# Cached attention keys: loaded in 128-byte runs and turned in 32x32 blocks on VectorE, in place of full transposes on TensorE

## What is computed

```python
def gather_pages(pool, page_table):      # pool: (n_phys, 128, 8 heads, 64)
    pages = pool[page_table]             # page_table: (8 sequences, 2 pages)
    b, n, p, h, d = pages.shape
    return pages.reshape(b, n * p, h, d)
...
k_all = jnp.concatenate([past_k.astype(dt), k_c], axis=1)     # 256 cached + 4 new positions
...
s = jnp.einsum('bhqd,bhqskd->bhqsk', qi, kg).astype(F32) * scale
p = jax.nn.softmax(s.reshape(B, H, qb, -1), axis=-1).reshape(s.shape)
return jnp.einsum('bhqsk,bhqskd->bhqd', p.astype(vg.dtype), vg)
```

## Time and profile before

| | us |
|---|---|
| three timed runs, median (lowest to highest) | 1137.73 (1137.03 to 1140.92) |
| profiled execution, span from first to last instruction | 1136.4 |
| TensorE busy | 1104.2 (97%) |
| VectorE busy | 696.0 (61%) |
| ScalarE busy | 353.0 (31%) |
| SP: cached keys, 32 DMAs of 256 KB, median to landing | 3.1 |

### The profile page before, as it was taken

How to read it: one execution, slowest core, us unless ns; L and a number is a source line. 1 busy time by engine, 2 the same in 40 slices (tenths; PEclk the granted TensorE clock), 3 DMA queues, 4 the chain that set the end, 5 groups by cost and what they waited for, 6 DMA issues and landing times.

```text
span 1136.4 us, 23106 instructions
## 1 busy us (share of the span) xinstructions
PE 1104.2 (97%) x8920; PEld 891.8 (78%) x8920; DVE 696.0 (61%) x1577; ACT 353.0 (31%) x809; POOL 129.3 (11%) x215
## 2 busy tenths in 40 slices
PE   7999999999999899999999999999999998999998
PEld 6778777768777598899977778777777876888997
DVE  4675546766666445567556673766667646463856
ACT  1242223322334153310323332233223332534013
POOL 0211402020211000000001123111102011000000
PEclk9999999999999999999999999999999998999999
DMA  8733236421513674454356331654134147544431
GB/s 262 222 112 117 58 102 211 100 75 40 137 52 112 179 264 150 139 164 131 110 157 177 112 99 41 189 164 94 39 91 117 58 129 237 187 152 149 149 112 42
DMA packets 162327, 148.57 MB, mean 131 GB/s; under 512 B 41512, under 2 KB 144526, under 8 KB 162028
## 3 DMA queue, kind: packets, MB, share of 16 engines
q1 hardware_dynamic: 156820, 135.99, 40.2%
q0 software_dynamic: 2848, 7.79, 2.0%
q10 hardware_dynamic: 2552, 3.32, 0.9%
HBM read 135.42 MB, written 11.07 MB: 129 GB/s over the span
## 4 chain that ended last, share of the span: by engine, by line
PE 88%; DVE 4%; SPq 2%; DMA 2%; issue 1%; ACT 1%; DVEq 0%; ACTq 0%
PE psum L1305 43%; PE psum L1346 10%; PE psum L1367 7%; PE psum L1233 5%; PE psum L1557 2%; PE psum L1574 2%; PE psum L1421 1%; PE psum L1432 1%; PE psum L1693 1%; SPq L1159 1%; DMA arena<-conv_in 1%; PE psum L1959 1%; PE psum L1908 1%; PE psum L1777 1%; PE psum L1938 1%
## 5 line engine op out<-in xcount | busy, mean ns | idle before, releaser
L1305 PE MATMUL psum<-x_b,ring 128*128 128x288 f32 x928 | 245.3, 414 | 0.0
L1305 PE MATMUL psum<-x_a,ring 128*128 128x288 f32 x928 | 243.8, 412 | 0.0
L1305 PEld LDWEIGHTS psum<-x_b,ring 128*128 128x128 f32 x928 | 171.4, 191 | 49.4 <-issue 6.5
L1305 PEld LDWEIGHTS psum<-x_a,ring 128*128 128x128 f32 x928 | 170.6, 191 | 49.0 <-issue 6.5
L2044 ACT ACTIVATE arena<-psum 128x512 f32<-128x512 f32 (+7 forms) x181 | 78.1, 451 | 172.6 <-PE psum L1233 62.7
L1305 PE MATMUL psum<-z,ring 128*128 128x288 f32 (+1 forms) x384 | 83.5, 368 | 0.0
L1305 PEld LDWEIGHTS psum<-z,ring 128*128 128x128 f32 x384 | 62.3, 190 | 12.8 <-issue 2.3
L2044 ACT ACTIVATE arena<-arena 128x256 f32<-128x256 f32 (+9 forms) x102 | 44.5, 465 | 62.5 <-DVE arena L3308 28.2
L1233 PE MATMUL psum<-consts,arena 128*128 128x128 f32 (+2 forms) x362 | 53.9, 281 | 7.3 <-DMA arena<-in_x_prompt 4.9
L1233 PEld LDWEIGHTS psum<-consts,arena 128*128 128x128 f32 (+2 forms) x362 | 42.9, 145 | 17.6 <-issue 6.3
L2044 ACT ACTIVATE triangles<-psum 128x512 f32<-128x512 f32 (+2 forms) x48 | 24.7, 515 | 77.2 <-PE psum L1557 58.8
(11 more groups left out here) (478 smaller groups left out, 1988.8 us busy)
## 6 DMA issues: line engine op xcount, KB each, us to landing
ring<-in_w_in SPq DMA_DIRECT2D x72, 1024.0 KB, 5.4
ring<-in_w_branch SPq DMA_DIRECT2D x12, 1024.0 KB, 5.7
arena<-in_cache_k SPq DMA_DIRECT2D x32, 256.0 KB, 3.1
arena<-in_cache_v SPq DMA_DIRECT2D x32, 256.0 KB, 3.7
ring<-in_w_out SPq DMA_DIRECT2D x8, 1024.0 KB, 5.1
ring<-in_w_pg SPq DMA_DIRECT2D x8, 1024.0 KB, 5.2
arena<-in_state_dn SPq DMA_DIRECT2D x8, 512.0 KB, 6.8
out_dn_sample<-arena POOLq DMA_DIRECT2D x8, 512.0 KB, 6.4
```

The lines of the kernel that those rows point to most:

```text
L1305: ins = mm(out[:, 0:n], lhs, rhs(k), start=k == 0, stop=k == k_tiles - 1)
```

## The change

- `c_fetch_k`: four DMAs for each page in place of one. DMA b puts channels 32b to 32b + 31 of each head pair on partitions 32b to 32b + 31; partition 32b + t takes positions 4t to 4t + 3, so every DMA has 32 partitions x 16 runs of 32 floats.
- `c_keys` leaves TensorE and ScalarE. On VectorE it is one `transpose` of 128x1024 in blocks of 32x32 from `CKR` to `CKT`. It signals `past_k_t`, on which SP's next fetch and TensorE's `c_past` wait; `past_k_ts` is gone. Its place in the list is the same.
- `c_past`: the keys' operand is read as 8 runs of 32 columns, and VectorE's copy of the scores restores the order of positions.
- The fetch of the values is unchanged (written out in place).

```diff
-    "past_k0_loaded": {"c_fetch_k": (32, lambda st: st[2] % 2 == 0)},
+    "past_k0_loaded": {"c_fetch_k": (128, lambda st: st[2] % 2 == 0)},
...
-        CKT = part(4, 4, 256)
+        CKT = part(4, 1024)
...
-            def fetch(cache, l, s, dst, name):
+            def page(l, s, pg):
+
+                return sp.value_load(PTAB[0:1, 2 * s + pg:2 * s + pg + 1], min_val=0, max_val=A["cache_k"].shape[1] - 1)
+
+            def fetch_blocks(l, s):
 
                 for pg in range(2):
-                    r = sp.value_load(PTAB[0:1, 2 * s + pg:2 * s + pg + 1], min_val=0,
-                                      max_val=A["cache_k"].shape[1] - 1)
-                    src = cache[l, bass.ds(r, 1), :, :, :].rearrange("o p h d -> (o p) (h d)")
-                    sp.dma_start(dst[:, pg, :], src).then_inc(S.sem(name), 16)
+                    src = A["cache_k"][l, bass.ds(page(l, s, pg), 1), :, :, :].rearrange("o (t a) h d -> t (o a h d)", a=4)
+                    for b in range(4):
+                        blocks_of = src.rearrange("t (m b d) -> b t m d", b=4, d=32)[b]
+                        dst = CKR[32 * b:32 * b + 32, s % 2, pg, :].rearrange("p (m d) -> p m d", d=32)
+                        sp.dma_start(dst, blocks_of).then_inc(S.sem(f"past_k{s % 2}_loaded"), 16)
...
-            def c_keys(l, g, j):
-                s = 4 * g + j
-                pe.wait_ge(S.sem(f"past_k{s % 2}_loaded"), S.count(f"past_k{s % 2}_loaded"))
...
+            def c_past(l, g):
+
+                pe.wait_ge(S.sem("past_k_t"), S.count("past_k_t"))
...
-                for pg in range(2):
-                    for pr in range(4):
-                        ins = tr(M[3 * (s % 2) + pg][:, 128 * pr:128 * pr + 128], CKR[:, s % 2, pg, 128 * pr:128 * pr + 128])
-                ins.then_inc(S.sem("past_k_t"), 1)
-
-            def c_past(l, g):
-
-                pe.wait_ge(S.sem("past_k_ts"), S.count("past_k_ts"))
...
-                        mm(M[2][32 * i:32 * i + 32, 0:256], CQX[:, pr, 4 * g + i, :], CKT[:, i, pr, :], start=pr == 0, stop=pr == 3,
-                           skip_group_check=True)
+                        keys = CKT[:, i, :].rearrange("p (g m n) -> p g m n", m=4, n=32)[:, :, pr, :]
+                        out = M[2][32 * i:32 * i + 32, 0:256].rearrange("p (g n) -> p g n", n=32)
+                        mm(out, CQX[:, pr, 4 * g + i, :], keys, start=pr == 0, stop=pr == 3, skip_group_check=True)
...
-            def c_keys(l, g, j):
-                s = 4 * g + j
-                act.wait_ge(S.sem("past_k_t"), S.count("past_k_t"))
-
-                act.wait_ge(S.sem("c_ssc"), S.count("c_ssc"))
-                for pg in range(2):
-                    ins = fn(CKT[:, j, :, 128 * pg:128 * pg + 128], v4(M[3 * (s % 2) + pg], 128), ACT.Copy)
-                ins.then_inc(S.sem("past_k_ts"), 1)
-                act.wait_ge(S.sem("past_k_ts"), S.count("past_k_ts"))
...
+            def c_keys(l, g, j):
+                s = 4 * g + j
+                dve.wait_ge(S.sem(f"past_k{s % 2}_loaded"), S.count(f"past_k{s % 2}_loaded"))
+                dve.wait_ge(S.sem("c_ssc"), S.count("c_ssc"))
+                dve.transpose(CKT[:, j, :], CKR[:, s % 2].rearrange("p g n -> p (g n)")).then_inc(S.sem("past_k_t"), 1)
+
             def c_past(l, g):
                 dve.wait_ge(S.sem("c_ssc"), S.count("c_ssc"))
-                cp(CPS[:, 0:256], M[2][:, 0:256])
+                cp(CPS[:, 0:256].rearrange("p (g n a) -> p g n a", g=2, a=4), M[2][:, 0:256].rearrange("p (g a n) -> p g n a", g=2, a=4))
```

More of the change, by code:

```diff
@@ L134 @@
     "rw_state_loaded": {"b_scale": (256, lambda st: st[3] == 0)},
-    "past_k0_loaded": {"c_fetch_k": (32, lambda st: st[2] % 2 == 0)},
-    "past_k1_loaded": {"c_fetch_k": (32, lambda st: st[2] % 2 == 1)},
+    "past_k0_loaded": {"c_fetch_k": (128, lambda st: st[2] % 2 == 0)},
+    "past_k1_loaded": {"c_fetch_k": (128, lambda st: st[2] % 2 == 1)},
     "past_v0_loaded": {"c_fetch_v": (32, lambda st: st[2] < 4)},
@@ L240 @@
     "past_k_t": {"c_keys": (1, None)},
-    "past_k_ts": {"c_keys": (1, None)},
     "projected": {"p_a": (1, None), "p_z": (1, None), "p_ba": (1, None), "p_f": (1, None), "p_c": (1, None), "p_g": (1, None), "p_up": (1, None), "p_end": (1, None), "w_y": (1, None), "w_pg": (1, None), "w_g": (1, None), "p_ple": (1, None), "c_rms": (1, None), "b_shiftout": (1, None)},
@@ L868, in program @@
         GTC = part(3, NTOK)
-        PLN = CKT[:, :, :, :].rearrange("p a b n -> p (a b n)")[:, 0:3 * D_PLE].rearrange("p (a n) -> p a n", a=3)
+        PLN = CKT[:, :, :].rearrange("p a n -> p (a n)")[:, 0:3 * D_PLE].rearrange("p (a n) -> p a n", a=3)
         CPS = CP.rearrange("p a b -> p (a b)")[:, 0:NTOK]
@@ L1183, in c_fetch_k @@
                     sp.wait_ge(S.sem("past_k_t"), S.count("past_k_t"))
-                fetch(A["cache_k"], l, s, CKR[:, s % 2], f"past_k{s % 2}_loaded")
+                fetch_blocks(l, s)
             def c_fetch_v(l, s):
@@ L1194, in c_fetch_v @@
                     sp.wait_ge(S.sem("c_so_s"), S.count("c_so_s"))
-                fetch(A["cache_v"], l, s, CVR[:, s % 4], f"past_v{s // 4}_loaded")
+                for pg in range(2):
+                    src = A["cache_v"][l, bass.ds(page(l, s, pg), 1), :, :, :].rearrange("o p h d -> (o p) (h d)")
+                    sp.dma_start(CVR[:, s % 4, pg, :], src).then_inc(S.sem(f"past_v{s // 4}_loaded"), 16)
             def y_out(l, m):
@@ L1925, in c_keys @@
                 pe.wait_ge(S.sem("c_done"), S.count("c_done"))
-                pe.wait_ge(S.sem("c_sdone"), S.count("c_sdone", S.at - 1))
+                pe.wait_ge(S.sem("c_sdone"), S.count("c_sdone"))
                 pe.wait_ge(S.sem("c_max"), S.count("c_max", S.at - 1))
-                for pg in range(2):
-                    for pr in range(4):
-                        ins = tr(M[3 * (s % 2) + pg][:, 128 * pr:128 * pr + 128], CKR[:, s % 2, pg, 128 * pr:128 * pr + 128])
-                ins.then_inc(S.sem("past_k_t"), 1)
-            def c_past(l, g):
-                pe.wait_ge(S.sem("past_k_ts"), S.count("past_k_ts"))
                 for pr in range(4):
                     for i in range(4):
-                        mm(M[2][32 * i:32 * i + 32, 0:256], CQX[:, pr, 4 * g + i, :], CKT[:, i, pr, :], start=pr == 0, stop=pr == 3,
-                           skip_group_check=True)
+                        keys = CKT[:, i, :].rearrange("p (g m n) -> p g m n", m=4, n=32)[:, :, pr, :]
+                        out = M[2][32 * i:32 * i + 32, 0:256].rearrange("p (g n) -> p g n", n=32)
+                        mm(out, CQX[:, pr, 4 * g + i, :], keys, start=pr == 0, stop=pr == 3, skip_group_check=True)
                 for pr in range(4):
@@ L2006, in _ @@
                       b_fin=b_fin, b_norm5=b_norm5, c_rms=c_rms, c_rope=c_rope, c_nat=c_nat, c_score=c_score,
-                      c_prob=c_prob, c_pv=c_pv, c_out=c_out, c_keys=c_keys, c_past=c_past, c_sprob=c_sprob, c_spv=c_spv, c_sout=c_sout, y_out=y_out, y_end=y_end)
+                      c_prob=c_prob, c_pv=c_pv, c_out=c_out, c_past=c_past, c_sprob=c_sprob, c_spv=c_spv, c_sout=c_sout, y_out=y_out, y_end=y_end)
             for i, st in enumerate(order):
@@ L2514, in _ @@
                       b_exp=b_exp, b_pairs=b_pairs, bs_pairs=bs_pairs, b_nat=b_nat, bs_nat=bs_nat, bs_inv=bs_inv, b_u=b_u, b_fin=b_fin, b_norm2=b_norm2, b_norm4=b_norm4,
-                      c_sq=c_sq, c_rms=c_rms, c_nat=c_nat, c_score=c_score, c_past=c_past, c_prob=c_prob, c_keys=c_keys, c_sprob=c_sprob, c_spv=c_spv)
+                      c_sq=c_sq, c_rms=c_rms, c_nat=c_nat, c_score=c_score, c_past=c_past, c_prob=c_prob, c_sprob=c_sprob, c_spv=c_spv)
             for i, st in enumerate(order):
@@ L3384, in _ @@
                       bs_scale=bs_scale, bs_pairs=bs_pairs, bs_in=bs_in, bs_sq=bs_sq, bs_w=bs_w, bs_u=bs_u, bs_y=bs_y, bs_out=bs_out,
-                      c_turn=c_turn, c_rope=c_rope, c_score=c_score, c_prob=c_prob, c_pv=c_pv, c_out=c_out, c_past=c_past, c_sout=c_sout,
+                      c_turn=c_turn, c_rope=c_rope, c_score=c_score, c_prob=c_prob, c_pv=c_pv, c_out=c_out, c_keys=c_keys, c_past=c_past, c_sout=c_sout,
                       y_out=y_out)
```

1 line of the change is left out of this document (removed).

## The result

| | before | after |
|---|---|---|
| median of the timed runs | 1138.8 us (4 runs) | **1171.35 us** (1168.5 to 1172.1, 4 runs) |
| span of the profiled execution | 1136.4 us | 1166.7 us |
| that execution's own time | 1137.73 us | 1168.5 us |

The ratio is **1.0276** (95%: 1.0254 to 1.0298): 32.5 us slower. The forecast had the sign, with +15.5 us (1153.2 beside 1137.73), and the time lies above its range (1139 to 1166).

The account below looks back on a forecast made before the run. TensorE, busy in 97% of the span, was taken to bound the kernel. Span 1136.4 + 12.1 (late c_past, removed transposes included) + 3.4 (clock) = 1151.9; with 1.3 to the median, 1153.2 us, range 1139 to 1166.

Parts of the forecast that it names:

- The account by halves: Late keys delay c_past in each layer by 1.9 us in the first half and 4.15 in the second, together +12.1.
- SP's time for a key DMA: Issue of a 512-run key DMA on SP: 0.535 us from start to start, bounds 0.34 and 1.0.
- The page number's own 0.56: Reading the second page number on SP adds 0.56 us to each sequence's key fetch.
- The third rival: SP's cost grows with the runs: 1.0 us a key DMA, +29.8 us, 1183 us; chance 0.07.
- Removed from TensorE, added to VectorE: Key transposes: 14.2 us leave TensorE, all on the path; 16 of 1.245 us, 19.9 in all, go to VectorE.
- Landing and packets: Key DMAs land 2.2 us after issue; a 128 B packet takes 13.4 ns, so engines need 3.4 us per sequence.
- Where TensorE stops: TensorE idles before c_past, 3.7 us in first halves and 3.1 in second, and some 1.5 at product 4 in first halves.
- +4.15 for a second half: c_past of sequences 4 to 7 starts at 484.45 instead of 480.30, behind an idle stretch of 3.1 us.
- The clock: TensorE at half clock after two of four new stops of 3 to 4 us: +3.4 us, bounds 0 and 10.8.
- Cover on SP: The 16 x 3.1 us added on SP hide in its waits for TensorE, with four weight chunks in the ring as cover.

Follow-up runs that it names:

- Experiment 5: The changed kernel with keys fetched from fixed pages, so no page number or address arithmetic on SP for keys; 1152.64 us, ratio 1.0117.
- experiment 1: The changed kernel with the key loads put back to one DMA of 128 rows of 2 KB per page; 1131.24 us, ratio 0.9912.
- experiment 8: The changed kernel with key fetches sent earlier into free slots, those of sequences 2 and 3 ahead of the value loads; 1131.30 us, ratio 0.9928.
- experiment 10: The changed kernel with early key fetches as in experiment 8, c_keys(5) ten fillers later, and value pages issued by GpSimd instead of SP; 1129.85 us, ratio 0.9900.

## Why the prediction was right in sign and wrong in size

**The account by halves.** From the end of c_keys(0) or (4), which releases the fetch, to the start of c_past, the forecast had 422.85 - 407.55 = 15.3 us and 484.45 - 470.4 = 14.05. The trace has 21.4 and 17.9 in layer 0 and 20.2 and 17.9 in layer 1, 18.7 us more in all. In the same stretches SP took for the two fetches (chunk included) 16.7, 14.0, 16.1 and 14.0 us; the forecast's own steps give 10.8 (408.31 to 419.09) and 10.3. That is 18.6 us more. So one term carries the miss: **SP's time for a key DMA**. Some 14 us of it (64 DMAs x 0.22) are the steady price of a DMA; about 5 us, 4.4 of them in the first halves, are single DMAs that took up to 1.6 us, most at a DMA share of 0.83 to 0.85; the forecast had no term for them. All that lies outside these four stretches came out 3.9 us better than forecast, and 18.7 - 3.9 is the 14.8 us between the forecast's span, 1151.9, and 1166.7.

**What was wrong in that term.** I took 0.535 us from start to start out of bounds of 0.34 and 1.0; it is 0.754. Experiment 5, at 0.67 without arithmetic, parts the 0.22 us of the error. First, the list (0.135): the earlier trace rows had 451 ns and a start-to-start time of 0.48 at 256 runs, and I gave "a little", 0.055, for twice as many; like for like, with fixed addresses, it is 627 ns and 0.67 at 512, 0.7 ns for each further run. With computed addresses the runs show 316 ns at 32 rows, 338 at 128 rows and 563 at 512 runs. 338 and 451 stood in the earlier trace rows already, and a line through them goes to 677 at 512. Second, the address arithmetic (0.084): I took the start-to-start time of the states' DMAs (0.48), which have fixed addresses, for keys whose address is computed. The pair of page DMAs had the arithmetic in its 1.37 us, and I didn't look for it there. The page number's own 0.56 was right: in the change two DMAs with one between them start 1.32 us apart, 0.57 more than without.

**The third rival was the neighbour.** It had 1.0 us a DMA and 1183 us. Between 0.535 (1153.2) and 1.0 the line gives 1167 for 0.754; the measured time is 4 us above. The mechanism of that rival, a cost that grows with the runs, was half true, and it had a chance of 0.07. The range took its upper end from 0.535 and a little more, not from the 1.0 that the text itself called the bound; with that honoured, the range would have held the time.

**Removed from TensorE, added to VectorE:** right. 16 transposes at 1237 ns (19.9 us forecast, 19.6 measured), and much of TensorE's 14.2 us is there once the loads are out of the way: experiment 1 gains 9 in the median and 5.3 in the profiled spans. By the latter 6.2 of the 14.2 went to more idle time (stops of 2.5, 0.9 and 2.8 us before c_past and twice 1.5 behind VectorE remain, others are shorter) and 2.7 to slower work.

**Landing and packets:** right. 2.4 us from issue to landing for 2.2. In this stretch of the changed kernel, with little but keys in it, 0.48 x 16 x 8.00 us over 75 GB/s x 8.00 us / 128 B is 13.1 ns a packet; the forecast had 13.4.
```profile
1054.00:1062.00 8.00, 3.86 (x24) 3.30 (x22) 1.44 (x2) 0.38 (x1) 0.00 (x0) 0.89 0.48 75
```
The Trainium skill's sum of beats and three bus cycles ("DMA: Bandwidth & Descriptors", "Why small descriptors are slow (HBM only)"), by an estimate 8.2 ns, is not what the trace shows. It didn't matter: in the second halves keys came at SP's pace, with the engines busy for a share of 0.42 to 0.48.

**Where TensorE stops:** right in kind. It stops before each c_past (4.1, 3.3, 2.8 and 4.3 us, for 3.7 and 3.1), and at product 4. There the forecast named 1.5 us, in the first half alone; it was 5.5 and 5.0 in first halves and 3.7 and 3.9 in second ones. The forecast's own +4.15 for a second half, with 4 x 0.89 us taken away, asks for 7.7 us of stops, and it named 3.1: the sum by the keys was right, the list of stops wasn't.

**The clock:** the term was 3.4, and the forecast looked for two dips. The page's busy time shows 12.8 us of slower work, in more stretches than two. An estimate from the granted clock, busy time times the missing share of the clock in windows of 1 us, grows from 6.8 us before to 21.8, by 15.0: the clock alone is enough for it. Behind the stop that ended at 426.78, and behind that which ended at 488.29 (columns as in the earlier trace rows, then):
```profile
425.50:432.00 6.50, 5.22 (x69) 3.32 (x70) 2.81 (x6) 0.04 (x1) 0.00 (x0) 0.50 0.47 73
487.50:491.00 3.50, 2.71 (x11) 2.71 (x12) 0.73 (x2) 0.38 (x1) 0.00 (x0) 0.50 0.48 75
```
But much of it cost nothing: between a release and c_past the keys set the time, whatever TensorE's clock, and the second row lies there. From c_past to the next half's release it took 51.1 and 50.2 us where the forecast's own times give 49.5, and from the last c_past to the end 100.6 where it took 98.7: together 4.3 us, close to the term. The trace agrees with the two levels that the Trainium skill gives ("TensorE: Matmul & The Clock Gate", "Part 1"), 0.50 and 1.00 of 2.4 GHz.

**Cover on SP:** right. TensorE waited for no weight chunk in the changed kernel. But the cover was spent faster than forecast: two fetches took SP 13.98 us beside 4.04 in the earlier trace rows, 5.0 more for each sequence and not 3.1. All of SP's waits together fell by 60 us (904 to 844), where 49.6 were forecast, those for freed ring slots at the projections by 24 (beside the earlier trace rows):
```profile
SPq L1091 <- PE psum L1311: 595.8, 58, 24.8
```

## What to carry to other kernels

A DMA's price on its issuing queue is a term of its own: count it as DMAs x (issue at that number of runs + the address arithmetic between two with a computed address), and set that against the time from a buffer's release to the keys' first use, not against the queue's idle share. Where fetches follow each other on one queue, its time for them adds up and the landing counts once. Here 10 us more of SP for each pair of fetches cost 40 us of the end, in second halves with the DMA engines more than half idle; the same DMAs sent earlier, into free slots, cost nothing that can be told (experiments 1 and 8). And where a text gives a term two bounds, the range has to be carried to both ends.

## What the runs showed of the hardware

- SP's time for one DMA, with a computed address: 316 ns at 32 rows of 2 KB, 338 at 128 rows of 2 KB, 563 at 512 runs of 128 B. With a fixed address and DMAs back to back: 451 at 256 runs of 128 B, 627 at 512. So the address arithmetic, 0.19 us, costs 0.08 net.
- Single DMAs of the same form took SP up to 2.5 us in a stretch where the DMA engines' share was 1.14 (experiment 10: 20.8 us for sixteen, beside 14.5 in experiment 8 at a share of 0.87).
- A VectorE 32x32 transpose of 128x1024 took 1.20 to 1.25 us in all sixteen places; a matmul operand in 8 runs of 32 columns cost the same as one of 256 in a row (382 ns).
- GpSimd's block DMAs took it 0.65 us each, SP's 0.56, but four of them issued at 406.8 had landed only by 415.9, and one was held for 4.15 us with no releaser shown. The DMA engines' share was 1.21 there, for 229 GB/s; it was 0.85 for 241 GB/s with SP as the only issuer of keys.
